# Splitting the first gated rows inside the last block of the up product

## The chip, the cores and the metric
One core of one Trainium2 chip runs the whole program. The metric is the device time of one execution in microseconds. Five engines appear in the profile: TensorE (matmuls PE, weight loads PEld), VectorE (DVE), ScalarE (ACT), GpSimd (POOL) and SyncE (SP), which issues DMAs. They run side by side and wait for one another on semaphores; each works through its own instructions in order.

## The reference
Two transformer-like layers over a sequence of 512 tokens of width 1024 are computed one after the other. Each ends with a feed-forward of hidden width 2816, and these two are what the change touches:

```
first:   a, b = split(h @ w_up)             # 1024 -> 2 x 2816
         x += g2 * ((silu(conv3(a)) * b) @ w_down)   # conv3: depthwise, 3 taps along the tokens, with bias
second:  a, b = split(h @ w_in)
         x += g2 * rmsnorm((silu(a) * b) @ w_out)    # 2816 -> 1024
```

Apart from these there are adaptive-norm vectors (`c_act @ ada_w`), a neighbourhood attention with a state-space mixer, and a windowed attention. The vector product for the second layer (`ada_w_2`, 24 pieces) is computed on VectorE, piece by piece, between the other work of the first feed-forward.

## The kernel before
Activations are held transposed: 128 partitions by 512 tokens for each chunk of 128 features. To get float32 accuracy, each operand is split in two parts, high and low, and each product is three matmuls: high x high, high weight x low input, low weight x high input (`chunk_products`, L245; in the down product `down_products`, L284). Weights come in blocks of 128x2048 (1 MB), two buffers deep: SyncE loads a block to `w_raw` (L222), ScalarE copies it, rounded, to `w_hi` (`high`, L229), GpSimd subtracts in four pieces of 512 columns to make `w_lo` (`low`, L238). `high` for block b waits until block b-2 has been used up.

The input of the up product, eight chunks, is in `h_hi` and `h_lo`, split likewise. A block of the up product makes two tiles of 128x512 in two PSUM banks: first the half that goes through Silu, then the half it is multiplied with. Each tile takes 8 chunks x 3 = 24 matmuls; a feed-forward has 22 such blocks: two in `lead`, twenty in a loop of ten turns (`rest`, `tiles`). Banks 0 and 1 serve the even blocks, 2 and 3 the odd ones.

For each block ScalarE (`glu`) and VectorE gate the two tiles. In the first feed-forward: ScalarE scales the first tile with the middle tap and adds the bias (L1334), VectorE adds the two outer taps (`outer_taps`, L1443 and L1445), ScalarE takes Silu (L1337); meanwhile VectorE adds one piece of the ada product (`add_ada2`, eight small operations at L1432 and L1434), and then multiplies with the second tile into `HID` (L1603). In the second feed-forward there are no taps and no ada: Silu (L1339), multiply (L1699). After each gate ScalarE issues `high` for the block after the next. In the last turn that is the second block of the down product, whose buffer comes free only when the up product has ended.

The down product uses all eight PSUM banks and takes `HID` in pairs of chunks, eleven pairs, one block of weights (48 matmuls) each. A pair is split like everything else: ScalarE copies it to two slots of `h_hi` (`hidden_high`, L1346), VectorE subtracts into the same slots of `h_lo` (`hidden_low`, L1610). Pair 0 takes slots 0 and 1, pair 1 slots 2 and 3, and so on in turn. These are the buffers of the up product's own input, so the first two pairs wait until the up product has ended. TensorE waits ahead of the down product for `tile_free` (all banks of the up product read) and then for each pair's `g_split`.

What the loops of the other engines run: SyncE loads blocks and ada pieces by turns, each waiting for its slot (L222, L213); the first feed-forward's last two ada pieces are added during the down product.

Of the kernel before, what the change touches and what calls it, by code (L numbers as in the profile page):

```python
# [6 lines left out]
ALU = mybir.AluOpType  # L7
ACT = mybir.ActivationFunctionType
# [6 lines left out]
DC = D // P  # L15
S = 512
# [17 lines left out]
B_IN, B_OUT, B_UP, B_DOWN = 0, 12, 16, 38  # L34
B_QKV, B_O, B_UP2, B_DOWN2, B_END = 49, 55, 59, 81, 92
# [58 lines left out]
def build(nc, T):  # L94

    es = ExitStack()
    with es:
# [3 lines left out]
        def sem(name):  # L101
            return es.enter_context(nc.semaphore(name))

        ps = [es.enter_context(nc.psum_tensor(f"bank{i}", [P, 512], F32)) for i in range(8)]
# [3 lines left out]
        h_hi = sb("h_hi", [P, DC, S], F32R)  # L108
# [68 lines left out]
        brow_done, brow_sb, brow_out, copies_out = sem("brow_done"), sem("brow_sb"), sem("brow_out"), sem("copies_out")  # L177
        bias_in, bias2_in = sem("bias_in"), sem("bias2_in")
        down_done, down_free = sem("down_done"), sem("down_free")
        g_hi, g_split = sem("g_hi"), sem("g_split")  # L180
        out_ready, out_done = sem("out_ready"), sem("out_done")
        yn_done, xr_odd, out_odd = sem("yn_done"), sem("xr_odd"), sem("out_odd")
# [41 lines left out]
        def high(act, b, off=0):  # L224

            act.wait_ge(raw_in[b % 2], 16 * (b // 2 + 1) + off * 8)
            if b >= 2:
                act.wait_ge(half_used, 2 * (b - 1) + 2 * off)
            nc.scalar.activation(w_hi[b % 2][:], w_raw[b % 2][:], ACT.Copy).then_inc(hi_done, 1)  # L229
# [18 lines left out]
        def products(pe, b, ft, bank, off=0):  # L248

            if ft == 0:  # L250
                pe.wait_ge(lo_done, b + 1 + off)
            for k in range(DC):
                last = chunk_products(b, ft, bank, k)
            last.then_inc(half_used, 1)
# [805 lines left out]
        def _(pe):  # L1060
# [97 lines left out]
            def tiles(b0, f0, turns):  # L1158

                with pe.Fori(0, turns) as i:  # L1160
                    for n in range(4):
                        pe.wait_ge(tile_free, f0 + n - 3 + 4 * i)
                        products(pe, b0 + n // 2, n % 2, ps[n], 2 * i)

            def lead_half(k0, k1):
                for k in range(k0, k1):
                    for n in range(4):
                        chunk_products(B_OUT + n // 2, n % 2, ps[n], k)

            def rest(b0, f0, turns):  # L1170
                tiles(b0 + 2, f0 + 4, turns - 1)
# [27 lines left out]
            spread(pe, 2, 4).then_inc(scale_out, 1)  # L1199
            pe.wait_ge(tile_free, F_UP)  # L1200
            lead(pe, B_UP, 8)
            rest(B_UP, F_UP, 11)
            pe.wait_ge(tile_free, F_QKV)
            down(B_DOWN, 0)

# [37 lines left out]
            spread(pe, 5, 5).then_inc(scale_out, 1)  # L1243
            pe.wait_ge(tile_free, F_UP2)
            lead(pe, B_UP2, 24)
            rest(B_UP2, F_UP2, 11)
            pe.wait_ge(tile_free, F_UP2 + 44)
            down(B_DOWN2, 11)
            mean(pe, 6, SQ2, 4)
# [4 lines left out]
        def _(act):  # L1254
# [68 lines left out]
            attention1_act(act)  # L1323
            ssd_act(act)

            def glu(b0, f0, taps0, silu0):

                with act.Fori(0, 11) as i:
                    for u in range(2):
                        act.wait_ge(tile_free, f0 + 2 * u - 2 + 4 * i)  # L1330
                        act.wait_ge(half_used, 2 * b0 + 2 * u + 1 + 4 * i)
                        if taps0 is not None:
                            j = 2 * i + u
                            nc.scalar.activation(HB2[:, u, :], ps[2 * u][:, :], ACT.Identity, bias=fconv[:, 3, bass.ds(j, 1)],  # L1334
                                                 scale=fconv[:, 1, bass.ds(j, 1)]).then_inc(tap_done, 1)
                            act.wait_ge(tile_free, f0 + 2 * u + 1 + 4 * i)
                            nc.scalar.activation(HB2[:, u, :], HB2[:, u, :], ACT.Silu).then_inc(tap_silu, 1)  # L1337
                        else:
                            nc.scalar.activation(HB2[:, u, :], ps[2 * u][:, :], ACT.Silu).then_inc(tap_silu, 1)  # L1339
                        high(act, b0 + u + 2, 2 * i)  # L1340

            def hidden_high(b0, t, off=0):

                act.wait_ge(half_used, 2 * b0 + (2 * (t - 1) if t >= 2 else 0) + 2 * off)
                src = HID[:, bass.ds(2 * t + 2 * off, 2), :]
                nc.scalar.activation(h_hi[:, 2 * (t % 2):2 * (t % 2) + 2, :], src, ACT.Copy).then_inc(g_hi, 1)  # L1346

            def down_act(b0, f_end):
                hidden_high(b0, 0)
                hidden_high(b0, 1)  # L1350
                act.wait_ge(tile_free, f_end)
                high(act, b0 + 2)
                with act.Fori(0, 4) as i:
                    for t in (2, 3):
                        hidden_high(b0, t, 2 * i)
                        high(act, b0 + t + 1, 2 * i)
                hidden_high(b0, 10)
# [5 lines left out]
                    high(act, B_OUT + n // 2 + 2)  # L1363
            root(act, 2, 4)
            affine(act, 1, lambda c: gain2[:, c:c + 1], lambda c: modb[:, 8 + c:9 + c], XN2, HB2)
            glu(B_UP, F_UP, 14, 14)
            down_act(B_DOWN, F_QKV)
            high(act, 49)
            high(act, 50)
# [27 lines left out]
                squares(act, 5, f, XR[:, f, :], SQ2)  # L1397
            root(act, 5, 5)
            affine(act, 3, lambda c: gain4[:, c:c + 1], lambda c: mod2[:, 24 + c:25 + c], XN2, HB2)
            glu(B_UP2, F_UP2, None, 36)  # L1400
            down_act(B_DOWN2, F_UP2 + 44)
            for f in range(DC):
                act.wait_ge(down_free, 8 + f + 1)
# [5 lines left out]
        def _(dve):  # L1409
# [14 lines left out]
            def add_ada2(j, off=0):  # L1424

                s = j % 2
                dve.wait_ge(ada_in[s], 16 * ((24 + j) // 2 - 3) + 8 * off)
                dst = acc2[:, bass.ds(256 * j + 256 * off, 256)]
                for k in range(8):
                    src = ada[:, s * BLK + k * 256:s * BLK + (k + 1) * 256]  # L1430
                    if k == 0:
                        link(nc.vector.tensor_scalar(dst, src, silu_c2[:, 0:1], None, ALU.mult))  # L1432
                        continue
                    ins = nc.vector.scalar_tensor_tensor(out=dst, in0=src, scalar=silu_c2[:, k:k + 1], in1=dst,  # L1434
                                                         op0=ALU.mult, op1=ALU.add)
                    if k < 7:
                        link(ins)
                    else:
                        ins.then_inc(ada_used, 1)

            def outer_taps(buf, src, w, m, n, done):

                link(nc.vector.scalar_tensor_tensor(out=buf[:, 1:n], in0=src[:, 0:n - 1], scalar=w[:, 0, m], in1=buf[:, 1:n],  # L1443
                                                    op0=ALU.mult, op1=ALU.add))
                nc.vector.scalar_tensor_tensor(out=buf[:, 0:n - 1], in0=src[:, 1:n], scalar=w[:, 2, m], in1=buf[:, 0:n - 1],  # L1445
                                               op0=ALU.mult, op1=ALU.add).then_inc(done, 1)
# [144 lines left out]
            dve.wait_ge(scale_out, 3)  # L1591
            normalise(dve, 1, XR, XN2, HB2, 4)

            with dve.Fori(0, 11) as i:
                link.loop(i, 2 * 8)
                for u in range(2):
                    j = 2 * i + u
                    dve.wait_ge(tap_done, 14 + u + 1 + 2 * i)
                    outer_taps(HB2[:, u, :], ps[2 * u], fconv, bass.ds(j, 1), S, tile_free)
                    add_ada2(u, 2 * i)  # L1600
                    dve.wait_ge(tap_silu, 14 + u + 1 + 2 * i)
                    dve.wait_ge(half_used, 2 * B_UP + 2 * u + 2 + 4 * i)
                    nc.vector.tensor_tensor(HID[:, bass.ds(j, 1), :].rearrange("p a n -> p (a n)"), HB2[:, u, :], ps[2 * u + 1][:, :],  # L1603
                                            ALU.mult).then_inc(tile_free, 1)
                link.end(11)

            def hidden_low(g0, t, off=0):
                dve.wait_ge(g_hi, g0 + t + 1 + off)
                part = slice(2 * (t % 2), 2 * (t % 2) + 2)
                nc.vector.tensor_tensor(h_lo[:, part, :], HID[:, bass.ds(2 * t + 2 * off, 2), :], h_hi[:, part, :],  # L1610
                                        ALU.subtract).then_inc(g_split, 1)

            def down_dve(g0, with_ada):
                hidden_low(g0, 0)
                hidden_low(g0, 1)
                if with_ada:
                    add_ada2(22)
                    add_ada2(23)
                with dve.Fori(0, 4) as i:
                    hidden_low(g0, 2, 2 * i)  # L1620
                    hidden_low(g0, 3, 2 * i)
                hidden_low(g0, 10)
# [69 lines left out]
            scale_of(dve, 5)  # L1692
            dve.wait_ge(scale_out, 7)
            normalise(dve, 3, XR, XN2, HB2, 5)
            with dve.Fori(0, 11) as i:
                for u in range(2):
                    dve.wait_ge(tap_silu, 36 + u + 1 + 2 * i)
                    dve.wait_ge(half_used, 2 * B_UP2 + 2 * u + 2 + 4 * i)
                    nc.vector.tensor_tensor(HID[:, bass.ds(2 * i + u, 1), :].rearrange("p a n -> p (a n)"), HB2[:, u, :],  # L1699
                                            ps[2 * u + 1][:, :], ALU.mult).then_inc(tile_free, 2)  # L1700
            down_dve(11, False)
            for f in range(DC):
                dve.wait_ge(*((down_done, 7 + f + 1) if f < DC - 1 else (half_used, 2 * B_END)))
# [122 lines left out]
```

## Time and profile before

| | us |
|---|---|
| median of 3 runs | 1539.46 (1539.35 to 1541.57) |
| profiled execution | 1537.85 |
| its span | 1536.0 |
| TensorE busy | 1411.0 (92%) |
| VectorE / GpSimd / ScalarE busy | 652.5 / 637.8 / 559.0 |
| mean granted clock of TensorE | 0.945 |

The two up products run from 508 to 752 and from 1150 to 1391 us of the span, the down products behind them to 879 and 1517. In a matmul row the duration is modelled, and matmuls overlap; the distance between two starts is what one costs. A number behind x is a count. In the chain of waits "issue" is time in which the engine waited for nothing that the profile shows.

### The profile page before, as it was taken

The numbers are of one execution on the slowest core, as the hardware profiler recorded it, in microseconds if no ns is written. First come the engines' busy times: TensorE is split into PE (matmuls) and PEld (weight loads), VectorE is DVE, ScalarE is ACT, GpSimd is POOL, SyncE is SP. The second block draws the span as 40 slices with busy tenths as digits, with TensorE's granted clock in tenths as the row PEclk, the third lists the DMA queues.
The fourth block names the chain that finished last, engine by engine and source line by source line (L and its number), as shares of the span: only waits on it lengthen the run. The fifth ranks groups of instructions, "written<-read, shape, count | busy, mean of one in ns | idle before, by whom it ended". The sixth has DMA issues, their size and how long they took to land.

```text
span 1536.0 us, 17809 instructions
## 1 busy us (share of the span) xinstructions
PE 1411.0 (92%) x6432; PEld 1134.7 (74%) x6432; DVE 652.5 (42%) x1173; ACT 559.0 (36%) x810; POOL 637.8 (42%) x516
## 2 busy tenths in 40 slices
PE   8699997898678899999899989999979999998995
PEld 1588867686676678888788888655868888887884
DVE  1564578676833665455611163466242000001115
ACT  2502313463312544434322351476234232232221
POOL 0233354134634254444455445433333454534542
PEclk9799997899889899999999969999969999999998
DMA  9124553600013145545522232200111223232221
GB/s 394 55 103 168 198 197 107 153 1 1 1 55 125 69 186 198 215 183 199 191 82 84 80 137 82 83 1 1 55 55 55 109 82 109 82 109 79 86 82 55
DMA packets 26977, 165.42 MB, mean 108 GB/s; under 512 B 2688, under 2 KB 4992, under 8 KB 8496
## 3 DMA queue, kind: packets, MB, share of 16 engines
q1 hardware_dynamic: 24912, 150.10, 26.6%
q10 hardware_dynamic: 2016, 14.68, 2.6%
q8 instruction: 29, 0.48, 0.1%
q14 instruction: 20, 0.16, 0.0%
HBM read 162.64 MB, written 6.32 MB: 110 GB/s over the span
## 4 chain that ended last, share of the span: by engine, by line
PE 82%; DVE 7%; issue 4%; POOL 4%; ACT 2%; DMA 1%; POOLq 0%; DVEq 0%; SPq 0%; ACTq 0%
PE bank L245 45%; PE bank L284 16%; PE bank L1088 3%; PE bank L582 2%; PE bank L562 2%; PE bank L1066 2%; PE bank L443 2%; POOL arena L760 1%; PE bank L1209 1%; POOL arena L762 1%; PE bank L1148 1%; PE bank L572 1%; PE bank L422 1%; PE bank L423 1%; PE bank L1238 1%
## 5 line engine op out<-in xcount | busy, mean ns | idle before, releaser
L238 POOL TENSOR_TENSOR w_lo<-w_raw,w_hi 128x512 fp32r<-128x512 f32 x368 | 502.8, 1397 | 697.7 <-ACT w_hi L229 673.9
L245 PE MATMUL bank<-h_hi,w_hi 128*128 128x512 f32 x1120 | 444.1, 396 | 22.5 <-POOL w_lo L238 8.6
L245 PE MATMUL bank<-h_lo,w_hi 128*128 128x512 f32 x1120 | 440.0, 393 | 0.0
L245 PE MATMUL bank<-h_hi,w_lo 128*128 128x512 f32 x1120 | 439.5, 392 | 0.0
L229 ACT ACTIVATE w_hi<-w_raw 128x2048 fp32r<-128x2048 f32 x92 | 176.2, 1915 | 445.9 <-PE bank L284 173.3
L245 PEld LDWEIGHTS bank<-h_hi,w_hi 128*128 128x128 f32 x1120 | 213.2, 190 | 70.6 <-issue 17.2
L245 PEld LDWEIGHTS bank<-h_hi,w_lo 128*128 128x128 f32 x1120 | 212.7, 190 | 44.9
L245 PEld LDWEIGHTS bank<-h_lo,w_hi 128*128 128x128 f32 x1120 | 213.0, 190 | 44.1
L284 PE MATMUL bank<-h_hi,w_hi 128*128 128x512 f32 x352 | 138.9, 395 | 9.1 <-issue 9.1
L284 PE MATMUL bank<-h_hi,w_lo 128*128 128x512 f32 x352 | 138.6, 394 | 0.0
L284 PE MATMUL bank<-h_lo,w_hi 128*128 128x512 f32 x352 | 138.5, 393 | 0.0
L1699 DVE TENSOR_TENSOR arena<-arena,bank 128x512 f32 x22 | 15.1, 688 | 217.6 <-PE bank L245 217.6
L1610 DVE TENSOR_TENSOR h_lo<-arena,h_hi 128x1024 fp32r<-128x1024 f32 x22 | 33.2, 1518 | 172.9 <-ACT h_hi L1346 172.9
L1434 DVE SCALAR_TENSOR_TENSOR arena<-ada_ring,small,arena 128x256 f32 (+1 forms) x168 | 90.6, 539 | 6.0
L284 PEld LDWEIGHTS bank<-h_hi,w_hi 128*128 128x128 f32 x352 | 67.1, 191 | 23.8 <-issue 9.9
L1443 DVE SCALAR_TENSOR_TENSOR arena<-bank,params,arena 128x511 f32<-128x511 f32 (+1 forms) x36 | 25.4, 704 | 124.5 <-ACT arena L1334 92.0
L318 ACT ACTIVATE arena<-arena 128x512 f32<-128x512 f32 (+1 forms) x56 | 33.3, 598 | 123.1 <-DVE arena L1587 37.8
L284 PEld LDWEIGHTS bank<-h_hi,w_lo 128*128 128x128 f32 x352 | 67.0, 190 | 14.2
L284 PEld LDWEIGHTS bank<-h_lo,w_hi 128*128 128x128 f32 x352 | 67.1, 191 | 14.0
L718 POOL TENSOR_SCALAR arena<-arena,small 128x256 f32<-128x256 f32 (+1 forms) x64 | 32.8, 531 | 55.6 <-DVE small L676 55.6
L538 POOL TENSOR_SCALAR arena<-arena,small 128x512 f32<-128x512 f32 x32 | 21.7, 692 | 73.2 <-DVE small L517 73.2
L1088 PE MATMUL bank<-arena,w_raw 128*128 128x256 f32 x224 | 50.5, 379 | 0.0
(221 smaller groups left out, 1667.9 us busy)
## 6 DMA issues: line engine op xcount, KB each, us to landing
w_raw<-w_dram SPq DMA_DIRECT2D x92, 1024.0 KB, 4.9
ada_ring<-ada_dram SPq DMA_DIRECT2D x30, 1024.0 KB, 4.9
ada_ring<-ada_dram ACTq DMA_DIRECT2D x14, 1024.0 KB, 4.8
arena<-ada_dram SPq DMA_DIRECT2D x4, 1024.0 KB, 9.5
arena<-x_dram SPq DMA_DIRECT2D x2, 2048.0 KB, 11.6
bias_copies<-bias_rows SPq DMA_DIRECT2D x1, 4096.0 KB, 27.0
arena<-bias_copies SPq DMA_DIRECT2D x1, 3072.0 KB, 12.7
out_dram<-arena SPq DMA_DIRECT2D x8, 256.0 KB, 2.1
```

The source lines that it names most:

```text
L229: nc.scalar.activation(w_hi[b % 2][:], w_raw[b % 2][:], ACT.Copy).then_inc(hi_done, 1)
L238: last = nc.gpsimd.tensor_tensor(w_lo[b % 2][:, part], w_raw[b % 2][:, part], w_hi[b % 2][:, part], ALU.subtract)
L245: last = nc.tensor.matmul(bank[:, :], w[:, ft, k, :], x[:, k, :], start=k == 0 and m == 0, stop=k == DC - 1 and m == 2)
L284: last = nc.tensor.matmul(ps[f][:, :], w[:, k, f, :], x[:, 2 * gslot + k, :], start=first and k == 0 and m == 0, stop=last_block and k == ...
L318: nc.scalar.activation(buf[:, k % 2, 0:n], src, ACT.Square).then_inc(sq_done, 1)
L443: last = nc.tensor.matmul(ps[7][:, 0:256], v, pt1[G % 2][:, kb, :], start=kb == 0, stop=kb == 3)
L562: nc.tensor.matmul(ps[u % 3][:, 0:128 * (hi - lo)], q2[:, 2 * g + hq // 2, t * 128:(t + 1) * 128], k2[:, g, hq % 2, lo * 128:hi * 128], st ...
L582: last = nc.tensor.matmul(ps[7][:, :], vtok2[:, lo + kb, g, :], pt2[:, G % 2, kb, :], start=kb == 0, stop=kb == hi - lo - 1)
L718: nc.gpsimd.tensor_scalar(prob2[:, u % 8, 0:w], prob2[:, u % 8, 0:w], row_inv[:, u % 16:u % 16 + 1], 1.0, ALU.mult, ALU.mult).then_inc(s[" ...
L1088: last = nc.tensor.matmul(ps[4 + n % 2][:, 0:CTX], raw[:, n % 2, k, :], HC[:, k, :], start=k == 0, stop=k == DC - 1)
L1434: ins = nc.vector.scalar_tensor_tensor(out=dst, in0=src, scalar=silu_c2[:, k:k + 1], in1=dst, op0=ALU.mult, op1=ALU.add)
L1610: nc.vector.tensor_tensor(h_lo[:, part, :], HID[:, bass.ds(2 * t + 2 * off, 2), :], h_hi[:, part, :], ALU.subtract).then_inc(g_split, 1)
```

## The change
The last block of the up product is taken out of the loop (`last_turn`; the loop has nine turns). It multiplies chunks 0 to 3 into both tiles, signals `low_chunks_read`, then finishes the first tile with chunks 4 to 7, then the second. ScalarE's and VectorE's gate loops have ten turns and two single gates behind them; between the last two stand the splits of pairs 0 and 1, whose slots are those of chunks 0 to 3. In the down product's part both are gone. The same is done in both feed-forwards; the matmuls and the values are the same.

```diff
+            def last_turn(b, f):
+
+                for n in (0, 1):
+                    pe.wait_ge(tile_free, f + n - 3)
+                    products(pe, b, n, ps[n])
+                pe.wait_ge(tile_free, f)
+                pe.wait_ge(lo_done, b + 2)
+                for k in range(4):
+                    for ft in (0, 1):
+                        last = chunk_products(b + 1, ft, ps[2 + ft], k)
+                last.then_inc(low_chunks_read, 1)
+                for ft in (0, 1):
+                    for k in range(4, DC):
+                        last = chunk_products(b + 1, ft, ps[2 + ft], k)
+                    last.then_inc(half_used, 1)
+
...
-            rest(B_UP, F_UP, 11)
+            tiles(B_UP + 2, F_UP + 4, 9)
+            last_turn(B_UP + 20, F_UP + 40)
...
+            def gate(b0, f0, conv_taps, u, i=0):
+
+                act.wait_ge(tile_free, f0 + 2 * u - 2 + 4 * i)
+                act.wait_ge(half_used, 2 * b0 + 2 * u + 1 + 4 * i)
...
+                high(act, b0 + u + 2, 2 * i)
+
+            def glu(b0, f0, conv_taps, n):
+
+                with act.Fori(0, 10) as i:
+                    gate(b0, f0, conv_taps, 0, i)
+                    gate(b0, f0, conv_taps, 1, i)
+                gate(b0, f0, conv_taps, 20)
+                for t in range(2):
+                    act.wait_ge(low_chunks_read, n)
+                    nc.scalar.activation(h_hi[:, 2 * t:2 * t + 2, :], HID[:, 2 * t:2 * t + 2, :], ACT.Copy).then_inc(g_hi, 1)
+                gate(b0, f0, conv_taps, 21)
...
             def down_act(b0, f_end):
-                hidden_high(b0, 0)
-                hidden_high(b0, 1)
                 act.wait_ge(tile_free, f_end)
                 high(act, b0 + 2)
...
+            def gated(u, i=0):
+
+                j, buf, bank = 2 * i + u, HB2[:, u % 2, :], 2 * (u % 2)
+                dve.wait_ge(tap_done, 14 + u + 1 + 2 * i)
+                outer_taps(buf, ps[bank], fconv, bass.ds(j, 1), S, tile_free)
+                add_ada2(u, 2 * i)
+                dve.wait_ge(tap_silu, 14 + u + 1 + 2 * i)
+                dve.wait_ge(half_used, 2 * B_UP + 2 * u + 2 + 4 * i)
+                nc.vector.tensor_tensor(HID[:, bass.ds(j, 1), :].rearrange("p a n -> p (a n)"), buf, ps[bank + 1][:, :],
+                                        ALU.mult).then_inc(tile_free, 1)
+
+            with dve.Fori(0, 10) as i:
+                link.loop(i, 2 * 8)
+                gated(0, i)
+                gated(1, i)
+                link.end(10)
+            gated(20)
+            hidden_low(0, 0)
+            hidden_low(0, 1)
+            gated(21)
...
             def down_dve(g0, with_ada):
-                hidden_low(g0, 0)
-                hidden_low(g0, 1)
...
+            with dve.Fori(0, 10) as i:
+                gated2(0, i)
+                gated2(1, i)
+            gated2(20)
+            hidden_low(11, 0)
+            hidden_low(11, 1)
+            gated2(21)
             down_dve(11, False)
```

## Rows read from the trace of the kernel before

**Rows 1.** The page: shares of the span, a DMA issue (KB each, us to landing).
```profile
PE 1411.0 (92%) x6432; PEld 1134.7 (74%) x6432; DVE 652.5 (42%) x1173; ACT 559.0 (36%) x810; POOL 637.8 (42%) x516
...
w_raw<-w_dram SPq DMA_DIRECT2D x92, 1024.0 KB, 4.9
```

**Rows 2.** The chain of waits in order: start us, us, what.
```profile
544.70 201.65 PE bank L245 x888
...
756.33 122.46 PE bank L284 x528
...
1149.58 241.77 PE bank L245 x1056
...
1395.90 121.59 PE bank L284 x528
```

**Rows 3.** TensorE's waits: us in total, times, longest us.
```profile
PE bank L284 <- issue: 9.1, 2, 4.6
...
PE bank L422 <- issue: 2.9, 1, 2.9
```

**Rows 4.** Timeline, first seam: start us, us, engine, line, operation, count, [idle before, releaser].
```profile
743.01 5.33 POOL L238 TENSOR_TENSOR w_lo<-w_raw,w_hi 128x512 fp32r<-128x512 f32 x4 [5.86 <-ACT w_hi L229]
...
746.51 0.78 ACT L1334 ACTIVATE arena<-bank,params 128x512 f32<-128x512 f32 x1 [3.67 <-PE bank L245]
...
747.45 0.75 DVE L1443 SCALAR_TENSOR_TENSOR arena<-bank,params,arena 128x511 f32<-128x511 f32 x1 [3.42 <-ACT arena L1334]
...
749.15 0.63 ACT L1337 ACTIVATE arena<-arena 128x512 f32<-128x512 f32 x1 [1.85 <-DVE arena L1445]
...
749.41 3.61 DVE L1434 SCALAR_TENSOR_TENSOR arena<-ada_ring,small,arena 128x256 f32 x7
...
751.38 0.39 PE L245 MATMUL bank<-h_hi,w_lo 128*128 128x512 f32 x1
...
751.80 1.91 ACT L229 ACTIVATE w_hi<-w_raw 128x2048 fp32r<-128x2048 f32 x1 [2.02 <-PE bank L245]
...
752.93 0.68 DVE L1603 TENSOR_TENSOR arena<-arena,bank 128x512 f32 x1
...
753.62 1.99 ACT L1346 ACTIVATE h_hi<-arena 128x1024 fp32r<-128x1024 f32 x2
...
753.87 5.70 POOL L238 TENSOR_TENSOR w_lo<-w_raw,w_hi 128x512 fp32r<-128x512 f32 x3 [5.53 <-ACT w_hi L229]
...
754.15 0.35 SPq L222 DMA_DIRECT2D w_raw<-w_dram  x1
...
754.69 3.74 DVE L1610 TENSOR_TENSOR h_lo<-arena,h_hi 128x1024 fp32r<-128x1024 f32 x2 [1.08 <-ACT h_hi L1346]
```

**Rows 5.** Timeline, second seam.
```profile
1385.94 0.60 ACT L1339 ACTIVATE arena<-bank 128x512 f32<-128x512 f32 x1 [3.52 <-PE bank L245]
...
1390.95 0.39 PE L245 MATMUL bank<-h_hi,w_lo 128*128 128x512 f32 x1
...
1391.51 0.69 DVE L1699 TENSOR_TENSOR arena<-arena,bank 128x512 f32 x1 [10.20 <-PE bank L245]
```

**Rows 6.** Windows: stretch, its length, busy us (count) per engine, clock, DMA share, GB/s.
```profile
754.00:756.00 2.00, 0.00 (x0) 0.00 (x0) 1.31 (x1) 1.61 (x2) 2.00 (x2) 0.71 0.86 270
762.00:764.00 2.00, 2.00 (x11) 1.61 (x10) 1.86 (x5) 0.00 (x0) 0.00 (x0) 1.00 0.94 311
1394.00:1396.00 2.00, 0.10 (x1) 0.13 (x2) 1.74 (x2) 1.18 (x2) 2.00 (x2) 1.00 0.00 0
```

**Rows 7.** VectorE's line L1610: ns shortest/median/longest.
```profile
L1610 DVE TENSOR_TENSOR h_lo<-arena,h_hi x22: 1389/1422/2301, 754.7 to 1498.6; 128x1024 fp32r<-128x1024 f32 x22
```

**Rows 8.** Timeline, the gate loop's first turn.
```profile
524.54 5.43 DVE L1434 SCALAR_TENSOR_TENSOR arena<-ada_ring,small,arena 128x256 f32 x7
...
526.88 5.48 POOL L238 TENSOR_TENSOR w_lo<-w_raw,w_hi 128x512 fp32r<-128x512 f32 x4 [20.38 <-ACT w_hi L229]
...
527.14 2.83 DVE L1434 SCALAR_TENSOR_TENSOR arena<-ada_ring,small,arena 128x256 f32 x2
```

More of the change, by code:

```diff
@@ L179, in build @@
         down_done, down_free = sem("down_done"), sem("down_free")
+        low_chunks_read = sem("low_chunks_read")
         g_hi, g_split = sem("g_hi"), sem("g_split")
@@ L1245, in _ @@
             lead(pe, B_UP2, 24)
-            rest(B_UP2, F_UP2, 11)
+            tiles(B_UP2 + 2, F_UP2 + 4, 9)
+            last_turn(B_UP2 + 20, F_UP2 + 40)
             pe.wait_ge(tile_free, F_UP2 + 44)
@@ L1324, in _ @@
             ssd_act(act)
[L1326 to L1340, printed above, removed]
+            def gate(b0, f0, conv_taps, u, i=0):
+                act.wait_ge(tile_free, f0 + 2 * u - 2 + 4 * i)
+                act.wait_ge(half_used, 2 * b0 + 2 * u + 1 + 4 * i)
+                buf, bank = HB2[:, u % 2, :], ps[2 * (u % 2)]
+                if conv_taps:
+                    j = 2 * i + u
+                    nc.scalar.activation(buf, bank[:, :], ACT.Identity, bias=fconv[:, 3, bass.ds(j, 1)],
+                                         scale=fconv[:, 1, bass.ds(j, 1)]).then_inc(tap_done, 1)
+                    act.wait_ge(tile_free, f0 + 2 * u + 1 + 4 * i)
+                    nc.scalar.activation(buf, buf, ACT.Silu).then_inc(tap_silu, 1)
+                else:
+                    nc.scalar.activation(buf, bank[:, :], ACT.Silu).then_inc(tap_silu, 1)
+                high(act, b0 + u + 2, 2 * i)
[8 more added lines that the diff above has]
+                gate(b0, f0, conv_taps, 21)
             def hidden_high(b0, t, off=0):
@@ L1365, in _ @@
             affine(act, 1, lambda c: gain2[:, c:c + 1], lambda c: modb[:, 8 + c:9 + c], XN2, HB2)
-            glu(B_UP, F_UP, 14, 14)
+            glu(B_UP, F_UP, True, 1)
             down_act(B_DOWN, F_QKV)
@@ L1399, in _ @@
             affine(act, 3, lambda c: gain4[:, c:c + 1], lambda c: mod2[:, 24 + c:25 + c], XN2, HB2)
-            glu(B_UP2, F_UP2, None, 36)
+            glu(B_UP2, F_UP2, False, 2)
             down_act(B_DOWN2, F_UP2 + 44)
@@ L1592, in _ @@
             normalise(dve, 1, XR, XN2, HB2, 4)
[L1594 to L1605, printed above, removed]
             def hidden_low(g0, t, off=0):
@@ L1694, in _, with gated2 @@
             normalise(dve, 3, XR, XN2, HB2, 5)
[L1695 to L1700, printed above, removed]
+            def gated2(u, i=0):
+                dve.wait_ge(tap_silu, 36 + u + 1 + 2 * i)
+                dve.wait_ge(half_used, 2 * B_UP2 + 2 * u + 2 + 4 * i)
+                nc.vector.tensor_tensor(HID[:, bass.ds(2 * i + u, 1), :].rearrange("p a n -> p (a n)"), HB2[:, u % 2, :],
+                                        ps[2 * (u % 2) + 1][:, :], ALU.mult).then_inc(tile_free, 2)
+            with dve.Fori(0, 10) as i:
[5 more added lines that the diff above has]
+            gated2(21)
             down_dve(11, False)
```

## The prediction

> **What bounds the kernel now.** I read the page first: TensorE is busy 92% of the span, the next engine 42% [rows 1]. So only time in which TensorE stands still, or runs at half clock, is worth anything. The second view is the chain of waits in order of time [rows 2]. It shows each feed-forward as one long stretch of L245 matmuls (the up product), a short "issue" piece, and one long stretch of L284 matmuls (the down product). Within the stretches nothing else ends a wait: 888 matmuls in 201.65 us is 0.2271 us each, the full clock. The third view, TensorE's waits, sizes the seam: L284 waited twice, 9.1 us together, 4.6 at most [rows 3]. The fourth is the timeline of the two seams.
>
> First seam [rows 4]: the last up matmul starts at 751.38 and the first down matmul at 756.33 [rows 2]. Between them stands a row of steps on three engines. ScalarE waits for the end of the up product to make w_hi (751.80, 1.91 us), and only then copies the first gated pair to h_hi (753.62). VectorE subtracts it into h_lo (754.69), TensorE starts. Second seam: the same, from 1390.95 [rows 5] to 1395.90 [rows 2]. After either seam TensorE runs at half clock for a while: the clock column reads 0.71 from 754 to 756 and is back at 1.00 by 762 [rows 6]. What that costs is in the chain: 528 matmuls at 0.2271 us are 119.9 us, but the down products took 122.46 and 121.59, so 2.6 us and 1.7 us are lost [rows 2].
>
> **What the change takes away.** The last up block (48 matmuls, 10.9 us) now runs input chunks 0 to 3 of both its tiles (24 matmuls), then chunks 4 to 7 of the first tile (12), then those of the second (12). Matmul count and work per matmul stay the same. With the last start at 751.38, the low chunks are read by the 24th matmul, whose start is 24 x 0.227 = 5.45 us earlier, 745.93. The first tile, ready there before, is now ready 12 x 0.227 = 2.7 us later. The two copies and two subtractions for the first two pairs go in front of the last tile's work on ScalarE and VectorE. So the splits (most of the 4.7 us from the last matmul's slot to 1395.90, for one) leave the seam, and with them the w_hi copy that stood in front of them. What is late next is in both cases the wait that stands ahead of the down product for all banks to be free, that is for the last gated multiply. The two feed-forwards differ in what stands before that multiply, so I work them separately.
>
> **Second feed-forward.** Before, ScalarE's Silu of the last gate starts at 1385.94; the copies can take that place. They end near 1388.0 (two took 1.99 us in the first seam [rows 4]), the subtractions follow one copy behind and end near 1389.8. The first tile is ready at about 1388.65, its Silu (0.60 us) done before the up product ends. The multiply needs the second tile and so stays where it is: 1391.51 plus 0.69 is 1392.20 [rows 5]. TensorE was 0.1 us behind its releaser in the old seam, so it starts at 1392.3 instead of 1395.90: **3.6 us sooner**. The idle stretch shrinks from 4.7 to about 1.1 us. The clock there was still 1.00 between 1394 and 1396, up to five us after the last up matmul's start [rows 6], so I expect no drop and the 1.7 us back as well. Bounds: 3.6 with the drop, 5.3 without; I take **5.3**. The w_hi copy for the second down block stays at the end of the up product, its w_lo follows in some 5 us, and the second down block needs it 10.9 us after the restart: hidden.
>
> **First feed-forward.** Here VectorE does two convolution taps on the first tile, then eight small adds of another product (L1432, L1434), then the multiply. In the trace this runs from 747.45 to 753.61: 5.48 us from first tap to the multiply's start, 0.68 for it [rows 4]. It hid inside the old seam; now it starts later and the bank wait exposes it.
> - Its start: the first copy can begin near 746.4, the first subtraction near 747.4, beside the last w_lo piece of GpSimd, which ends at 743.01 + 5.33 = 748.34. Two subtractions took 3.74 us with GpSimd busy beside both [rows 4]; the shortest of the 22 took 1.39 [rows 7], so two at least 2.8. From 747.4 that gives 750.2 to 751.1; I take 750.6, since one of the two is beside GpSimd. The first tap cannot start before the bias copy at 749.2 + 0.8 = 750.0 in any case.
> - Without anything new: 750.6 + 5.48 + 0.68 + 0.1 = 756.9, so TensorE starts 0.5 us later than now.
> - But the w_hi copy of the next block stands behind the Silu, which stands behind the taps. In the trace the taps' start to Silu's start is 1.70 us, Silu 0.63, the copy to GpSimd's start 753.87 - 751.80 = 2.07 [rows 4]. So GpSimd starts w_lo 4.3 us after the first tap, during the adds, where before it started after them. What that costs is shown by the first turn of the loop [rows 8]: GpSimd starts at 526.88, and the seven L1434 adds from 524.54 take 5.43 us instead of the 3.61 of [rows 4], the last two of them 2.83 us. GpSimd enters there in the same place of the sequence (526.88 - 524.54 = 2.3 us after the first of the seven; here 4.3 less the 1.96 from tap to that add, 2.3). So I add **1.8 us**.
>
> TensorE then starts at 758.7 instead of 756.33: **2.4 us later**. Bounds: 0.1 (subtractions at their shortest, no collision) and 3.8 (at their slowest, collision, and one add more caught, at 0.9). The half clock cost 2.6 us after this seam and 1.7 after the other [rows 2], with equal gaps, so its size is partly luck; I put its change at 0, with 1.6 us either way in the range.
>
> The Trainium skill bears on the collision ("SBUF — State Buffer", section "SBUF: two separate sides"): VectorE and GpSimd share a port pair as an exclusive lock held for a whole instruction, and a VectorE operation with two SBUF inputs takes it. The trace agrees: adds of 3.61 / 7 = 0.5 us last 1.4 us beside w_lo [rows 8], and the taps and the multiply, with one operand in PSUM, keep their 0.75 and 0.68 us. By the rule the adds do collide; without the lock the sum would be better by 1.8 us.
>
> **Other parts.** The weight and ada loads: the ada slot for the last add waits for the adds of the last tile, so its DMA is issued some 5 us later, and on SP's queue the weight load for the third down block stands behind it (754.15 before, about 759 now). Such a load lands in 4.9 us [rows 1], and is needed a down block after the restart, at 758.7 + 10.9 = 769.6: hidden. If that cover were gone it would cost what the load is late, us for us. The table loads of the gate stay as before in the peeled turn (ScalarE idles 3.67 us in front of a tile [rows 4]); a further pair behind the copies would be beside TensorE's last 24 matmuls and cost nothing. The peeled turns are straight-line code: price 0, since the chain has the straight-line lead block and the loop behind it in one piece, 1056 matmuls in 241.77 us [rows 2]; the other end is in the rivals.
>
> **Sum.** +2.4 - 5.3 = **-2.9 us**. The profiled execution took 1537.85 us (span 1536.0), so 1534.9 by its account; the median of the runs, 1539.46, lies 1.6 us above it, and against the median the forecast is **1536.5**. 0.2% is 3.1 us, about what can be told from no change; the forecast lies next to it.
>
> **Rivals.**
> - A, the forecast: the first seam grows, the second shrinks, net -2.9 (with clock luck -1.5 to -4.5). Chance 0.47; it falls on both sides of the 0.2% line, more often inside.
> - B, no collision or a shorter half-clock stretch in the first seam: +0.5 or less 1.6 of clock, net -4.5 to -5: 1534.7. For it: the start of w_lo against the adds is a matter of tenths. Against: both starts hang on the same tap, so they move together. 0.20.
> - C, the clock falls in the second seam all the same, after 1.1 us of idling: net +2.4 - 3.6 = -1.2, 1538.3. Against it the 1.00 in [rows 6]; for it, that it was down within 5 us of the last matmul in the first seam. 0.13.
> - D, slower: the peeled blocks are code that TensorE has not run, and it stops for it once in each, like the single 2.9 us "issue" wait before L422 [rows 3]. From 1.5 us each it eats the gain; at 2.9 each it is +5.8 - 2.9 = +2.9, 1542.4. Against it: the lead block, also 96 straight matmuls, shows none. 0.11.
> - E, both seams shrink alike, because the bank wait of the first is not last: -10.6, 1528.9. Against it the 6.2 us from tap to multiply. 0.04.
> The rest, 0.05, is for small mishaps near zero.
>
> Faster by over 0.2%: the smaller part of A (0.2), B and E: 0.44. Within: the larger part of A, C, some of the rest: 0.43. Slower: D and a remnant: 0.13. The range holds A, B and C and their run-to-run clock luck: 1532.8 to 1540.5.
>
> **What the changed profile would show.** The chain keeps two "issue" or VectorE pieces before L284: about 7 us at the first seam with the gated multiply as releaser, 1.1 us at the second. The L1434 adds before the first seam have two members of 1.4 us. The second down product takes 120 us, with clock 1.00 throughout. The forecast is wrong if the first seam is no longer than 5 us, if the clock drops in the second, or if TensorE pauses within the last up block.

## The result, and the profile after

| | before | after |
|---|---|---|
| median, us | 1539.63 (4 runs, 1539.35 to 1541.57) | 1530.97 (4 runs, 1530.20 to 1531.32) |
| profiled execution | 1537.85 | 1530.20 |
| span | 1536.0 | 1528.4 |
| mean granted clock | 0.945 | 0.948 |

The ratio is 0.9937, 95% interval 0.9919 to 0.9954: 8.7 us faster by the medians, 7.6 us by the two spans. The forecast was 2.9 us faster, 1536.5, range 1532.8 to 1540.5. The time lies below the range.

The chain of waits of the kernel after, in order of time (start us, us, what), against [rows 2]:

```profile
544.64 201.61 PE bank L246 x888
...
757.99 121.62 PE bank L285 x528
879.61 15.79 PE bank L1227 x96
...
906.57 66.05 PE bank L246 x288
...
1146.51 241.60 PE bank L246 x1056
...
1388.98 119.99 PE bank L285 x528
...
1512.74 2.09 PE bank L354 x8
```

And the pieces of the chain of the kernel before that the prediction did not use:

```profile
878.79 18.04 PE bank L1209 x96
...
908.19 67.28 PE bank L245 x288
...
1521.27 1.17 PE bank L353 x8
```

L1209 (L1227 after) is the sum of the ada product over the partitions, right behind the first down product: 48 float32 matmuls of one column each, which show as 96 records. I call them the column sums. The 288 matmuls are the second layer's first product. "Restart" is the first down matmul's start. The difference of the two chains, piece by piece, gives the whole 7.6 us:

| piece | us |
|---|---|
| up to the first up loop | -0.1 |
| loop start to first restart (211.63 to 213.35) | +1.7 |
| first down product (122.46 to 121.62) | -0.8 |
| its end to the start of the next product (29.40 to 26.96) | -2.4 |
| that product (67.28 to 66.05) | -1.2 |
| up to the second up product | -0.2 |
| second up product and seam (246.32 to 242.47) | -3.9 |
| second down product (121.59 to 119.99) | -1.6 |
| what follows it (L353, L354 after: 2.09 for 1.17) | +0.9 |

So the seams and down products together gave -4.6 us; 3.7 us (2.44 and 1.23 before rounding) came from a stretch that the change does not touch. The seams first. TensorE's waits name the releasers, both now VectorE's gated multiply:

```profile
PE bank L285 <- DVE arena L1635: 6.3, 1, 6.3
...
PE bank L285 <- DVE arena L1731: 0.9, 1, 0.9
```

The timeline of the first seam, VectorE (columns as in [rows 4]):

```profile
747.37 2.86 DVE L1624 TENSOR_TENSOR h_lo<-arena,h_hi 128x1024 fp32r<-128x1024 f32 x2 [5.06 <-ACT h_hi L1368]
750.15 0.74 DVE L1470 SCALAR_TENSOR_TENSOR arena<-bank,params,arena 128x511 f32<-128x511 f32 x1
...
751.97 5.37 DVE L1461 SCALAR_TENSOR_TENSOR arena<-ada_ring,small,arena 128x256 f32<-128x256 f32 x7
757.27 0.67 DVE L1635 TENSOR_TENSOR arena<-arena,bank 128x512 f32<-128x512 f32 x1
```

GpSimd in the same stretch:

```profile
754.29 5.46 POOL L239 TENSOR_TENSOR w_lo<-w_raw,w_hi 128x512 fp32r<-128x512 f32 x4 [6.28 <-ACT w_hi L230]
```

The subtractions start at 747.37 (forecast 747.4), the taps at 750.15 (forecast 750.6), GpSimd 4.1 us behind the first tap (forecast 4.3), and the seven adds take 5.37 us, as in [rows 8] and not the 3.61 of [rows 4]. TensorE restarts at 757.99 (forecast 758.7). The second seam in TensorE's timeline:

```profile
1387.71 0.39 PE L246 MATMUL bank<-h_hi,w_lo 128*128 128x512 f32 x1
1388.98 0.50 PE L285 MATMUL bank<-h_hi,w_hi 128*128 128x512 f32 x1 [0.88 <-DVE arena L1731]
```

1.3 us from start to start, where it was 4.95 [rows 2, 5], and the down product behind it ran at full clock: 119.99 us for 528 matmuls.

The windows show the stretch behind the first down product. Columns as in [rows 6]; the granted clock is the third number from the end. Before:

```profile
881.00:884.00 3.00, 3.00 (x17) 3.00 (x16) 2.60 (x5) 3.00 (x6) 1.47 (x2) 0.52 0.00 0
...
906.00:909.00 3.00, 1.50 (x6) 1.14 (x5) 1.83 (x4) 3.00 (x5) 0.00 (x0) 0.50 1.05 387
```

After:

```profile
881.00:884.00 3.00, 3.00 (x29) 3.00 (x28) 1.78 (x4) 3.00 (x6) 0.65 (x2) 1.00 0.00 0
...
906.00:909.00 3.00, 2.43 (x11) 1.99 (x12) 2.70 (x5) 3.00 (x5) 0.00 (x0) 1.00 1.06 428
```

The column sums start 0.8 us later than before, yet in the same three microseconds 29 of their records pass at 2.4 GHz where 17 passed, nearly all at 1.2 GHz. The clock falls later, and it is back at 1.00 by 906, before the next product starts; before, that product started at 0.50.

### The profile page after: what moved, and what is told of

The parts are those of the page before. It is cut to its first block, busy times and chain, and to the rows that moved or that the text cites. A ratio compares the mean times of both kernels' runs of the same rounds, so it can differ in the third digit from the quotient of the medians.

```text
span 1528.4 us, 17743 instructions
## 1 busy us (share of the span) xinstructions
PE 1406.1 (92%) x6432; PEld 1130.5 (74%) x6432; DVE 651.7 (43%) x1173; ACT 555.5 (36%) x807; POOL 634.2 (41%) x516
## 4 chain that ended last, share of the span: by engine, by line
PE 82%; DVE 7%; POOL 4%; issue 3%; ACT 2%; DMA 1%; POOLq 0%; SPq 0%; DVEq 0%; ACTq 0%
PE bank L246 46%; PE bank L285 16%; PE bank L1089 3%; PE bank L583 2%; PE bank L563 2%; PE bank L1067 2%; PE bank L444 2%; POOL arena L761 1%; PE bank L1227 1%; POOL arena L763 1%; PE bank L1149 1%; PE bank L573 1%; PE bank L423 1%; PE bank L424 1%; PE bank L354 1%
## 5 line engine op out<-in xcount | busy, mean ns | idle before, releaser
L1731 DVE TENSOR_TENSOR arena<-arena,bank 128x512 f32 (+1 forms) x22 | 15.2, 689 | 208.7 <-PE bank L246 208.7
```

## The experiments

All times are medians beside runs of the kernel before on the same chip; its median there was 1539.7, 1539.7 and 1539.8 in the three sessions. The chains are of one execution each. In these the first up loop starts anywhere from 544.3 to 550.8 us, though no edit changes the work ahead of it, so some microseconds of a difference in time can come from there. Distances from the loop's start are free of that. The question: do the parts add up, and is the 3.7 us in the untouched stretch an effect of the moment at which the first down product ends, or of the change itself?

**Each feed-forward alone.** In `ff2_only` the first feed-forward is as before, in `ff1_only` the second.

```diff
 # ff2_only
-            tiles(B_UP + 2, F_UP + 4, 9)
-            last_turn(B_UP + 20, F_UP + 40)
+            rest(B_UP, F_UP, 11)
...
 # ff1_only
-            tiles(B_UP2 + 2, F_UP2 + 4, 9)
-            last_turn(B_UP2 + 20, F_UP2 + 40)
+            rest(B_UP2, F_UP2, 11)
...
```

(and the gate loops and splits of that feed-forward as before)

> The change in the second feed-forward alone. Theory (parts add up; the clock behind the first down product depends on when that product ends): the second seam shrinks by the same 3.7 us and its half-clock stretch (1.6 us) goes, nothing else moves, so about 5.3 us faster than before, at least 4.3 us if the clock at the end of the kernel takes some back. Rival (the stretch after the first feed-forward gains whatever is done): 8 us or more.

> The change in the first feed-forward alone. Theory: the first seam grows by 1.7 us, its half-clock stretch costs 0.8 less, and the column sums and the first product of the second layer run at a better clock (about 3.7 us less), so 2 to 4 us faster than before, though the seam itself is longer. Rival (only seams count, as forecast): within 1 us of before, or slower by up to 2.4 us.

`ff2_only`: 1534.48, ratio 0.9966 (0.9951 to 0.9980), 5.2 us faster. Its chain has 3.7 us less in the second seam and 1.6 less in the down product behind it, and nothing behind the first; but 1.0 us is given back at the end, and its span is 3.9 us under before. That the medians give just the forecast's 5.3 is partly luck. `ff1_only`: 1537.11, ratio 0.9981 (0.9967 to 0.9995), 2.6 us faster, though its seam is as long as in the kernel after. Its chain (its start is 5.7 us later than after's already at the loop, so distances count):

```profile
550.31 201.66 PE bank L246 x888
...
763.71 121.76 PE bank L285 x528
...
912.41 66.04 PE bank L246 x288
```

Loop start to restart is 213.40, end of the down product (885.47) to next product 26.94, that product 66.04. The parts add up: 5.2 + 2.6 = 7.8 against 8.7. The rival of `ff2_only` falls. That of `ff1_only` (within 1 us of before) touches the interval, 0.8 to 5.1 us; the chain decides against it, since the 26.94 us and 66.04 us are those of the kernel after.

**The moment alone.** A few matmuls on constants, into a bank nobody reads, ahead of the first down product: more work, nothing else changed. My expectations for the first two priced such a float32 matmul at 0.22 us; it runs as two records, and records of that shape are 0.216 us apart in the kernel before (L1088, 3.45 us for 16), so at full clock one costs 0.43, four 1.7 and twelve 5.2. The edit below is that of `b_fill4`; `b_fill2` has two, `a_fill12` twelve on the kernel after.

```diff
+            pe.wait_ge(g_split, 1)
+            for _ in range(4):
+                nc.tensor.matmul(ps[7][:, 0:256], ident, con[:, 0:256], start=True, stop=True)
             down(B_DOWN, 0)
```

> The kernel before, with four extra 128x256 matmuls (0.22 us each at full clock) into an unused bank at the start of the first down product, so that it ends about 0.8 us later, as it does with the change. Theory (the clock behind it depends on that end alone): the column sums take 15.8 us instead of 18.0 and the next product starts at full clock, so the kernel with more work is about 3 us faster than before. Rival (the saving is an effect of the change itself): 0.9 us slower than before.

> The kernel after, with twelve such extra matmuls (2.6 us) at the start of the first down product. Theory: the column sums fall back to 18.0 us and the next product starts at half clock, so it loses 2.6 us and another 2.4 to 3.7 us, 5 to 6.3 us slower than the kernel after (about 1536). Rival (no dependence on the moment): 2.6 us slower than the kernel after (about 1533.5).

> The kernel before, with two extra 128x256 float32 matmuls (four passes, 0.86 us at full clock) at the start of the first down product, so that it ends when it does with the change. Theory (the clock behind the first down product depends on the moment of its end): column sums 15.8 us instead of 18.0, next product 1.2 us shorter, so about 2.5 us faster than before with more work in it. Rival: 0.9 us slower.

`b_fill2`: 1536.34, ratio 0.9977 (0.9959 to 0.9996), **3.3 us faster with 0.9 us more work**. Its chain:

```profile
758.53 2.05 PE bank L1206 x4
760.58 121.27 PE bank L284 x528
881.85 15.80 PE bank L1212 x96
...
908.79 66.01 PE bank L245 x288
```

The fillers took 2.05 us, the down product behind them 1.2 us less than before, so it ends 334.98 us behind the loop's start; before it was 334.09, after 334.97. The column sums take the 15.8 us of the kernel after, and end of down product to next product is 26.94, with nothing of the change in it. The rival falls.

`b_fill4`: 1539.72, ratio 0.9999 (0.9986 to 1.0013). 3 us faster was expected, and that was missed: with the fillers at twice the price the down product ends 1.8 us later than before and not 0.8, and the faster clock gives back 1.5 us of it. `a_fill12`: 1538.03, 7.1 us slower than the median after. Their column sums:

```profile
882.52 16.55 PE bank L1212 x96
```

```profile
886.53 17.45 PE bank L1230 x96
```

The expectation for `b_fill2` (2.5 us faster) was met. That for `a_fill12` (5 to 6.3 us slower) was missed, and both terms of its working were wrong: by its chain the first down product ends 5.3 us later behind the loop's start, where 2.6 was allowed, and the clock costs 1.2 us, where 2.4 to 3.7 was: the next product still took 66.02 us.

All fourteen profiled executions together, by when the first down product ends behind the loop's start (us), and how long it is from there to the start of the next product (us):

| kernels | its end | to the next product |
|---|---|---|
| `late_ada_sp` (below) | 328.5 | 26.95 |
| `late_ada` (below) | 330.3 | 28.16 |
| `order_only`, `order_again`, `mix` (below) | 331.6 | 26.94 to 26.95 |
| before, `ff2_only`, `late_high` (below) | 334.1 to 334.2 | 29.39 to 29.40 |
| after, `after_again`, `b_fill2`, `ff1_only` | 335.0 to 335.2 | 26.94 to 26.96 |
| `b_fill4` | 335.9 | 28.17 |
| `a_fill12` | 340.3 | 28.16 |

Kernels with different edits and the same end have the same figure, and 0.8 us between two ends is worth 2.4 us. Later is not better as such: the figure goes up and down. Nor is it the time since the kernel's start: in `b_fill4` and `after_again` the down product ends at 882.52 us alike.

The Trainium skill ("TensorE: Matmul & The Clock Gate", section "What's actually happening") says that the gate judges TensorE's activity on a count of its own that a kernel does not reset. The trace agrees so far that 0.9 us of shift changes where the clock falls; the count itself no run here shows, nor whether it is reset. I had not used it in the forecast.

**The first seam's two suspects.** In `late_high` ScalarE's last w_hi copy waits for the multiply; in `late_ada` the last tile's adds stand behind the multiply.

```diff
 # late_high
+                if u == 21 and conv_taps:
+                    act.wait_ge(tile_free, F_QKV)
                 high(act, b0 + u + 2, 2 * i)
 # late_ada
-            gated(21)
+            gated(21, ada=False)
+            add_ada2(21)
```

> The kernel after, but ScalarE waits for the last gated multiply of the first feed-forward before it makes w_hi of the second down block, so that GpSimd's w_lo comes after the adds and not beside them. Theory (GpSimd and the adds exclude each other): the adds keep 0.49 us each, the multiply starts 1.75 us sooner, TensorE restarts near 756.2 instead of 758.0, though another engine's work is made later; time 1.8 us less than after, within 3 us of clock luck. Rival (the two long adds have another cause): restart unchanged.

> The kernel after, with the last tile's eight ada adds in the first feed-forward moved from in front of its multiply to behind it. Theory (the chain taps, adds, multiply sets the first seam): taps end near 751.7, Silu near 752.3, multiply 753.0, TensorE restarts near 753.3 instead of 758.0, 4.7 us sooner, and with a seam of 1.5 us the clock does not fall, another 1.8 us; together 5 to 7 us faster than the kernel after (about 1525), give or take 3 us by the clock behind the first down product. Rival (the bank wait is not what ends last): restart unchanged within 0.5 us.

`late_high`, VectorE's timeline:

```profile
758.22 3.61 DVE L1463 SCALAR_TENSOR_TENSOR arena<-ada_ring,small,arena 128x256 f32<-128x256 f32 x7
761.75 0.68 DVE L1637 TENSOR_TENSOR arena<-arena,bank 128x512 f32<-128x512 f32 x1
```

Its chain:

```profile
550.80 201.69 PE bank L246 x888
...
762.48 122.53 PE bank L285 x528
885.01 18.00 PE bank L1227 x96
...
914.40 67.31 PE bank L246 x288
```

With GpSimd out of the way the adds are back at 3.61 us, and loop start to restart is 211.68, 1.7 us less than after, as expected. So the collision is shown, by taking it away; the rival falls. The time did not follow: 1534.86, ratio 0.9964 (0.9947 to 0.9981), 3.9 us **slower** than the first median of after, because the column sums went back to 18.0 us and the next product to 67.31. By the chains that is 3.7 us (29.39 and 67.31 for 26.96 and 66.05), and the down product took 0.9 more; less the 1.7, the chain gives 2.9 of the 3.9.

`late_ada`: 1530.97, ratio 0.9945 (0.9927 to 0.9963), the same as after; 5 to 7 us better was expected. The seam did what was expected, from TensorE's timeline:

```profile
755.94 0.50 PE L285 MATMUL bank<-h_hi,w_hi 128*128 128x512 f32 x1 [1.43 <-DVE arena L1636]
```

The loop starts at 547.50 there, so restart is 208.44 behind it, 4.9 us sooner, and the clock stays at 1.00 through the seam and behind it. But a new wait stands in the down product, from TensorE's waits:

```profile
PE bank L285 <- POOL w_lo L239: 1.6, 1, 1.6
```

and the column sums took 17.42 us instead of 15.79 (28.16 for 26.96 to the next product). From the loop's start to the end of the second layer's first product 3.5 us of the gain are left. They don't show in the time: in this execution the loop starts 2.9 us later than in the kernel after's. Whether that is chance stays open; none of its ten runs was under 1529.86. VectorE and SyncE in that stretch:

```profile
756.19 7.33 DVE L1461 SCALAR_TENSOR_TENSOR arena<-ada_ring,small,arena 128x256 f32<-128x256 f32 x7
```

```profile
763.55 0.33 SPq L214 DMA_DIRECT2D ada_ring<-ada_dram  x1
764.66 0.88 SPq L223 DMA_DIRECT2D w_raw<-w_dram  x2
```

The adds, now beside w_lo for longer, take 7.33 us; the last ada load waits for them; the third block's weights stand behind it on SyncE's queue. That is the queue the prediction went past as hidden; with the seam 4.9 us shorter it is not. `late_ada_sp` issues that weight load first:

```diff
-            for u in range(2):
-                load_block(sp, B_DOWN + u)
-                load_ada(sp, T["ada2"][22 + u], 46 + u)
+            load_block(sp, B_DOWN)
+            load_ada(sp, T["ada2"][22], 46)
+            load_block(sp, B_DOWN + 1)
+            load_block(sp, B_DOWN + 2)
+            load_ada(sp, T["ada2"][23], 47)
...
```

> The kernel with the adds of the last tile behind its multiply (late_ada), and on SyncE the load of the third down block issued ahead of the last ada load instead of behind it. Theory (in late_ada the ada load, which waits for the adds that GpSimd now slows, held up the weight load, and the third down block waited 1.6 us for w_lo): that wait goes, the first down product takes 120 us, so 1.6 us less than late_ada up to its end; with the clock behind it the time is 1526 to 1530. Rival (w_lo is late because GpSimd itself is slowed): the 1.6 us wait stays.

1524.76 (6 runs, 1522.97 to 1529.52), ratio 0.9911 (0.9894 to 0.9928): the fastest version, 14 to 15 us under before and 6 under after; two of its six runs were at 1529.4 and 1529.5. Its chain has the down product without a wait, and the better column sums:

```profile
544.27 201.61 PE bank L246 x888
752.75 119.99 PE bank L285 x528
872.74 16.07 PE bank L1230 x96
...
899.69 66.01 PE bank L246 x288
```

The rival (GpSimd itself too slow) falls: the wait is gone. Behind the loop's start this profile is 3.5 us shorter than `late_ada`'s; the other 3.2 of the 6.7 us between the two spans come from a loop that starts earlier (544.27 for 547.50).

**How much needs the early slots.** `order_only` is the kernel before with only ScalarE's order changed: the copies of both first pairs ahead of the last w_hi copy. `order_again` repeats it; `mix` has it in the first feed-forward and the full change in the second; `after_again` is the kernel after.

```diff
+                gate(b0, f0, taps0, 21, w_next=False)
...
                 hidden_high(b0, 0)
                 hidden_high(b0, 1)
+                high(act, b0 + 1)
                 act.wait_ge(tile_free, f_end)
```

> The kernel before, with one thing changed: in both feed-forwards ScalarE copies the first two pairs to h_hi ahead of the last w_hi copy instead of behind it; the up product's order is as before. Theory (the splits' place on ScalarE is part of the gain, and the rest needs the early slots): first restart near 754.9 instead of 756.3, since VectorE is free at 753.6; second near 1393.8 instead of 1395.9; 3.5 us faster than before. Rival (TensorE's order is what matters): no change.

> order_only once more, unchanged, with more runs. Theory: 9 to 10 us faster than before, equal to after within 1.5 us. Rival (its first six runs were lucky): 3.5 us faster than before.

> First feed-forward with only the order of ScalarE's copies changed (as in order_only), second with the full change. Theory (seams add up): first seam 1.6 us shorter than before, second 3.8 us, both without most of their half-clock loss, and the first down product ends where it does in order_only, so the column sums run at the better clock: 1.5 us faster than order_only, about 1528. Rival (the second seam's gain beyond order_only is hidden): the same as order_only.

> The kernel after, unchanged, on the chip of the two above, so that they can be compared. Theory: 8 to 9 us faster than before, as in its first runs.

| | median | ratio to before (95%) |
|---|---|---|
| `order_only` | 1529.59 | 0.9926 (0.9902 to 0.9951) |
| `order_again` | 1531.48 | 0.9946 (0.9933 to 0.9959) |
| `mix` | 1528.51 | 0.9927 (0.9914 to 0.9941) |
| `after_again` | 1531.27 | 0.9943 (0.9930 to 0.9956) |

The chain of `order_only`:

```profile
545.33 201.63 PE bank L245 x888
...
755.39 121.56 PE bank L284 x528
876.95 15.76 PE bank L1209 x96
...
903.90 66.02 PE bank L245 x288
...
1143.90 241.59 PE bank L245 x1056
...
1387.93 119.98 PE bank L284 x528
```

Its first seam is 1.6 us shorter than before (210.06 behind the loop's start; 1.4 expected), its second 2.3 us (244.03 for 246.32; 2.1 expected), and 3.5 us faster was expected. It got 10, and 8 in `order_again`, a little under the 9 to 10 expected there but equal to the kernel after, as expected: the rest is clock again, 0.9 and 1.6 us in the down products, 2.4 and 1.3 behind the first (15.76 for 18.04, 66.02 for 67.28). Swapping two steps of one engine is worth as much here as the whole change. The chains say how that comes about: in the first seam the reordering restarts TensorE 3.3 us sooner than the whole change does (210.06 for 213.35), in the second the whole change is 1.6 us better (242.47 for 244.03). `mix` takes the better of each: 3.0 us under `order_again` in the same session, where 1.5 was expected; its interval overlaps with that of `order_again`, and the chains account for 1.6. `after_again` repeats the first result, and stands beside `order_again` without a difference that can be measured.

## Why the prediction was wrong

- **Which wait is late next**: right in both seams, the gated multiply.
- **Second seam**, -3.6: it measured -3.9. **Its half clock**, -1.7: -1.6. `ff2_only` shows both in its chain, 3.7 and 1.6.
- **First seam**, +2.4: +1.7. The mechanism was right and the size 0.7 too large, most of it in the taps' start (750.15 for 750.6): the two subtractions took 2.86 us together, where I had allowed 3.2 with bounds of 2.8 and 3.7. **The collision**, +1.8, measured 5.37 - 3.61 = 1.8, and `late_high` shows its cause.
- **The change in the half clock, put at 0**: this is the step that failed. I priced half clock only where it stood behind a seam, called its size partly luck, and gave it 1.6 us either way. In the down product it gained 0.8, which that covers. But the column sums and the product behind them also ran at a clock that depends on when the down product ends, and the prediction had no term for them: 3.7 us together, with 0.9 us given back at the end of the kernel. Without these two the forecast's own terms, as measured, would have landed near 1535, inside the range. [rows 2] were read only as far as the down products. The next pieces of the same chain, 18.04 us for the column sums and 67.28 for 288 matmuls, which at 0.2271 us are 65.4, already showed a stretch that was not at full clock all through; 1.2 of the second's 1.9 us moved with it, and the other 0.7 is there at clock 1.00 too (66.05 after). `b_fill2` shows the cause: a shift of 0.9 us by idle work, and the same 3.7 us. Why the clock falls where it does, and which way a given shift will move it, the runs don't say.
- **SyncE's queue**: hidden, as said. But its cover was the long seam: `late_ada` removed that and paid 1.6 us.
- **The rivals**: C (clock falls in the second seam) and D (TensorE stops for peeled code) did not happen: the chain after has the 888 matmuls in 201.61 us and the 1056 in 241.60, as before, and its timeline shows starts 0.23 us apart to the end of the last up block. B (no collision, or less half clock behind the first seam) gave -4.5 to -5, which is what the forecast's own terms came to; its half clock came true by half (0.8 of 1.6), its missing collision didn't. E's place, the first seam shrinking like the second, did not happen either.

By the profile the forecast's own terms come to -4.6, where they said -2.9; -3.7 and +0.9 us it did not have, and -0.3 comes from small shifts. The profile gives 7.6 us (the parts are rounded) and the medians 8.7. The clock behind the first down product was profiled once in the kernel before and twice in the kernel after (15.79 and 15.77 us), so how often each meets the better one, and with it the last 1.1 us, stays open.

## What to carry to other kernels

When a buffer is freed early, ask what the next wait hangs on; where that is a chain with work of another purpose in it, move that work behind the multiply first, and then look which DMA queue was waiting for it. Before giving a shift of a microsecond no price, look through the chain for every stretch whose matmuls cost more than at full clock: each can move with it, up or down, by more than the edit itself. And try the small reordering before the restructuring.

## What the runs showed of the hardware that I had not expected

- The fall of the clock behind a dense stretch is sensitive to under a microsecond: the same column sums took from 15.8 to 18.0 us by when they began, and 0.9 us more work made the whole kernel 3.3 us faster.
- How long TensorE stood still: after 2.84 us from start to start across a seam (`order_only`'s second) the down product took 119.98 us, full clock; after its first, 3.39 us, it took 121.56, so the clock had fallen, as it had after both seams of 4.95 us before. The timeline of `order_only`'s second seam:

```profile
1385.09 0.39 PE L245 MATMUL bank<-h_hi,w_lo 128*128 128x512 f32 x1
1387.93 0.47 PE L284 MATMUL bank<-h_hi,w_hi 128*128 128x512 f32 x1 [2.45 <-issue]
```

- VectorE's small adds and GpSimd's subtractions take turns, one instruction each: 1.4 us an add instead of 0.5. In the 7.33 us of `late_ada` (3.61 undisturbed) that was so for four of seven, beside four pieces of w_lo in 5.59 us; 4 x 0.92 is the 3.7 between them.
